# Rotary embedding of differential attention: partner rows by DMA instead of a permutation product

## The chip, the core and the metric

The kernel runs on 1 core of one Trainium2 chip. The metric is the device time of one launch in microseconds (us). Engines are called PE (matrix products), DVE (vector), ACT (scalar), POOL (GpSimd) and SP (which here only issues DMAs).

## What is computed

Two transformer blocks in float32 run on 256 tokens of width 2048. The change touches the rotary embedding of the second block, in its differential attention. There q and k are split into heads of 64 features, and the first 16 features of each head are turned in pairs that stand 8 apart:

```
rot = d // 4; half = rot // 2                       # d = 64: rot = 16, half = 8
ang = pos[:, None] * inv_freq[None, :]
x1, x2 = xr[..., :half], xr[..., half:]
rotated = concatenate([x1 * cos(ang) - x2 * sin(ang), x2 * cos(ang) + x1 * sin(ang)], axis=-1)
```

The other 48 features pass unchanged. The rotated q and k then go into two softmax attentions whose difference weighs v; a stick-breaking attention stands beside it.

## The kernel before

All large products run on PE as three products of rounded halves: a weight tile is split into a high part (`high`, L1157, on ACT, from `raw` into `w_high_low`) and a low part (`low`, L1764, on DVE). A **tick** is one piece of 256 weight rows by 512 columns: SP loads it into one of 8 `raw` slots, ACT makes its high part, DVE its low part, and PE multiplies (`tick`, L508). Eight ticks, steps 0 to 7, make a **unit**. The high and low parts have 4 buffers, so ACT may make the high part of a tick when PE has finished the tick 4 before it; ACT and DVE therefore work 3 ticks ahead. At step s of unit n each of them first makes its part of the tick 3 later, and then does what the program hangs at (n, s). This order is written out by hand, and each engine keeps it: what hangs at a step holds up every later high or low part of that engine.

The 12 units of the q, k and v projection of the second block (`for n in range(12)`, L1057 on PE, L1661 on ACT, L2557 on DVE) come in two halves of four pairs of heads each. Units 0 and 6 give q of the differential attention, 1 and 7 its k, 2 and 8 its v, the rest q, k, v of the stick-breaking attention. Units 0 to 2 and 6 to 8 collect in the two large pairs of PSUM banks, `acc`, by turns; q and k come out with features on partitions ("cols" mode), v with tokens on partitions ("rows" mode). PE may begin unit n + 2 only when unit n's pair has been emptied (`acc_free`).

The rotary part before:
- `raw_epilogue(n)` (L1582, ACT) copies both banks of unit 0, 1, 6 or 7 into `diff_q_cols` or `diff_k_cols` at step 0 of the next unit.
- `rotate(n)` (L954, PE) multiplies that copy by the signed permutation `rotate` (L118), two products of 128x512 in float32 into the emptied `acc` pair. It hangs at step 1 of units 1, 2, 7 and 8.
- `rotary(n)` (L2429, DVE) multiplies the product by the sine table and the copy by the cosine table and adds; for k it writes `diff_k_halves`. It hangs at (1, 5) for q and (2, 1) for k in the first half, at (7, 1) and (8, 1) in the second, and frees the `acc` pair at its end.

The tables are scaled by one over the root mean square of each token at (1, 5) (`rotary_tables`, L2408), from a product of PE (`root_columns`, L947).

The attentions hang beside later units: differential heads at units 3 to 5 and 9 to 11, stick-breaking heads of the first half at units 6 to 8. At (3, 0) PE begins `diff_scores(0)` (L964, the products of L974 and L977), which waits for the `acc_free` that DVE gives after `half_copy` of unit 2 (L2192, its row has L2195, into `diff_v_rows`), at DVE's step 0 of unit 3. In the stick-breaking part PE turns each head's rows by `head_turn` (L1003, its rows have L1010), for which DVE's `normed` (L2478, rows L2481) must be done. For its second and fourth head of the first half `normed` hangs at (7, 4) and (8, 4) on DVE, and `head_turn` at (7, 5) and (8, 5) on PE, after that step's tick.

Of the kernel before, what the change touches and what calls it, by code (L numbers as in the profile page):

```python
# [12 lines left out]
P = 128  # L13
# [55 lines left out]

PORTIONS = [(0, 0, 4), (0, 4, 4), (1, 0, 2), (1, 2, 2), (1, 4, 4), (0, 8, 4), (1, 8, 4), (0, 12, 4), (1, 12, 4)]  # L70
# [32 lines left out]
def constants():  # L103
# [14 lines left out]
    rot = np.zeros((P, P), np.float32)  # L118
# [3 lines left out]
    for d in range(P):  # L122
        if d % 64 < 8:
            rot[d + 8, d] = -1.0
        elif d % 64 < 16:
            rot[d - 8, d] = 1.0
# [15 lines left out]
def build(nc, ins, out):  # L142
# [147 lines left out]
    RT = att("rotary_tmp", [P, 2, TOK])  # L290
# [5 lines left out]
    RD = at("root_diagonals", [P, NT, P], F32, placed["rotary_tmp"])  # L296
# [59 lines left out]
    rot_raw, rot_full = sem("rot_raw"), sem("rot_full")  # L356
# [150 lines left out]
    def _(pe):  # L507
# [636 lines left out]
    def _(act):  # L1144
# [437 lines left out]
        def raw_epilogue(n):  # L1582
# [1255 lines left out]
```

## Time and profile before

| | |
|---|---|
| time, median of 3 runs | 2066.51 us (2066.39 to 2069.49) |
| profiled execution: span from first to last instruction | 2065.7 us |
| its time as launched | not given apart; the span lies 0.8 us under the median |
| PE busy | 2030.8 us, 98% |
| DVE busy | 1301.5 us, 63% |
| ACT busy | 974.8 us, 47% |
| share of the chain that ended last | PE 90%, DVE 6%, ACT 2% |
| 16 DMA engines, queue of SP | 55.3% busy, 173 GB/s read from HBM |
| granted clock of PE | 0.998 of full speed |

How to read it: PE's ends are modelled and its products overlap, so its pace is read from the starts of its rows. Idle time of DVE or ACT costs nothing as long as PE finds its next operand ready. Where the chain of waits runs through DVE, PE had to stand.

### The profile page before, as it was taken

Reading aid. Unit: us, or ns where it says so; the run is one execution under the profiler, and the core shown is the slowest. Engines: PE = TensorE matmul, PEld = TensorE weight load, DVE = VectorE, ACT = ScalarE, POOL = GpSimd, SP = SyncE. Lnnn points to the kernel's source line nnn. Section 1 sums busy time; section 2 is a strip of 40 time slices with the busy share of each in tenths; the row PEclk is TensorE's granted clock in tenths of the full one; section 3 lists DMA queues with packets and bytes.
Section 4 is the critical chain, followed back from the end, with each engine's and each line's share of the span. In section 5 each row is a group of like instructions: output and inputs, shape, how many; then the busy total and the mean of one; then the engine's idle time right before and its main releaser. Section 6 shows DMA issues by size and latency. Waiting matters only on the chain.

```text
span 2065.7 us, 31956 instructions
## 1 busy us (share of the span) xinstructions
PE 2030.8 (98%) x12513; PEld 1788.3 (87%) x12513; DVE 1301.5 (63%) x1770; ACT 974.8 (47%) x1414; POOL 83.7 (4%) x84
## 2 busy tenths in 40 slices
PE   8999999999999999999999999999999999999998
PEld 7898898888989898889899898888888888888886
DVE  6799776456666666658666666556546555655655
ACT  5554554344444444446445546544434434434443
POOL 2000042000000000100000001000000000000000
PEclk9999999999999999999999999999999999999999
DMA  8245576545455554755554554666666666566663
GB/s 284 93 138 188 172 213 216 171 133 173 142 160 148 154 162 133 244 169 170 161 166 152 160 155 149 200 184 191 193 189 191 191 194 185 189 196 186 189 196 105
DMA packets 202935, 360.87 MB, mean 175 GB/s; under 512 B 25360, under 2 KB 33904, under 8 KB 202160
## 3 DMA queue, kind: packets, MB, share of 16 engines
q1 hardware_dynamic: 200656, 351.88, 55.3%
q0 software_dynamic: 1664, 5.97, 0.9%
q8 instruction: 99, 1.62, 0.3%
q10 hardware_dynamic: 480, 1.10, 0.1%
q14 instruction: 36, 0.29, 0.0%
HBM read 356.03 MB, written 2.10 MB: 173 GB/s over the span
## 4 chain that ended last, share of the span: by engine, by line
PE 90%; DVE 6%; ACT 2%; issue 2%; DMA 0%; ACTq 0%; POOL 0%; DVEq 0%; POOLq 0%
PE acc L517 35%; PE acc L521 19%; PE banks L517 8%; PE banks L1113 6%; PE acc L1113 6%; PE banks L1116 3%; PE acc L1116 3%; DVE w_high_low L1764 1%; PE acc L607 1%; ACT w_high_low L1157 1%; PE banks L882 1%; PE acc L548 1%; PE banks L910 1%; PE banks L999 1%; PE banks L977 1%
## 5 line engine op out<-in xcount | busy, mean ns | idle before, releaser
L1764 DVE TENSOR_TENSOR w_high_low<-raw,w_high_low 128x1024 fp32r<-128x1024 f32 x648 | 795.1, 1235 | 611.1 <-ACT w_high_low L1157 609.8
L1157 ACT ACTIVATE w_high_low<-raw 128x1024 fp32r<-128x1024 f32 x648 | 682.0, 1059 | 735.6 <-PE acc L517 329.7
L521 PE MATMUL acc<-x_high_low,w_high_low 128*128 128x256 f32 x3648 | 454.7, 285 | 0.7 <-issue 0.7
L521 PEld LDWEIGHTS acc<-x_high_low,w_high_low 128*128 128x128 f32 x3648 | 443.9, 192 | 3.5 <-issue 2.2
L517 PE MATMUL acc<-w_high_low,x_high_low 128*128 128x512 f32 x1728 | 413.9, 396 | 1.1 <-DVE w_high_low L1764 1.1
L517 PEld LDWEIGHTS acc<-w_high_low,x_high_low 128*128 128x128 f32 x1728 | 322.1, 188 | 68.2 <-issue 1.8
L517 PE MATMUL acc<-w_high_low,h_high 128*128 128x512 f32 x1088 | 292.6, 391 | 3.0 <-DVE w_high_low L1764 1.1
L517 PEld LDWEIGHTS acc<-w_high_low,h_high 128*128 128x128 f32 x1088 | 202.7, 188 | 45.9 <-issue 2.1
L517 PE MATMUL acc<-w_high_low,h_low 128*128 128x512 f32 x544 | 167.6, 389 | 0.0
L1113 PE MATMUL acc<-x_high_low,w_high_low 128*128 128x512 f32 x512 | 161.3, 396 | 1.5 <-DVE x_rows L2117 1.1
L1113 PE MATMUL banks<-x_high_low,w_high_low 128*128 128x512 f32 x512 | 160.8, 395 | 0.0
L517 PE MATMUL banks<-w_high_low,h_high 128*128 128x512 f32 x480 | 128.3, 389 | 0.0
L517 PEld LDWEIGHTS acc<-w_high_low,h_low 128*128 128x128 f32 x544 | 102.1, 188 | 21.4
L1116 PEld LDWEIGHTS banks<-x_high_low,w_high_low 128*128 128x128 f32 x512 | 96.2, 188 | 22.7
L1116 PEld LDWEIGHTS acc<-x_high_low,w_high_low 128*128 128x128 f32 x512 | 96.2, 188 | 22.7
L517 PEld LDWEIGHTS banks<-w_high_low,h_high 128*128 128x128 f32 x480 | 90.1, 188 | 18.7
L1116 PE MATMUL acc<-x_high_low,w_high_low 128*128 128x256 f32 x512 | 100.6, 278 | 0.0
L1116 PE MATMUL banks<-x_high_low,w_high_low 128*128 128x256 f32 x512 | 100.6, 278 | 0.0
L1113 PEld LDWEIGHTS acc<-x_high_low,w_high_low 128*128 128x128 f32 x512 | 78.3, 189 | 2.6 <-DVE x_rows L2117 1.3
L1113 PEld LDWEIGHTS banks<-x_high_low,w_high_low 128*128 128x128 f32 x512 | 77.9, 189 | 0.0
L517 PE MATMUL banks<-w_high_low,h_low 128*128 128x512 f32 x240 | 73.9, 389 | 0.0
L517 PEld LDWEIGHTS banks<-w_high_low,h_low 128*128 128x128 f32 x240 | 45.0, 188 | 9.4
(362 smaller groups left out, 1635.7 us busy)
## 6 DMA issues: line engine op xcount, KB each, us to landing
raw<-in_b_w_in SPq DMA_DIRECT2D x128, 512.0 KB, 3.8
raw<-in_w_mlp_in SPq DMA_DIRECT2D x128, 512.0 KB, 3.7
raw<-in_w_mlp_out SPq DMA_DIRECT2D x128, 512.0 KB, 4.5
raw<-in_w_in SPq DMA_DIRECT2D x96, 512.0 KB, 4.0
raw<-in_kv_w SPq DMA_DIRECT2D x48, 512.0 KB, 4.1
raw<-in_a_w_in SPq DMA_DIRECT2D x32, 512.0 KB, 6.3
raw<-in_b_w_out SPq DMA_DIRECT2D x32, 512.0 KB, 4.7
raw<-in_w_out SPq DMA_DIRECT2D x32, 512.0 KB, 4.6
```

The source lines that it names most:

```text
L517: ins_ = nc.tensor.matmul(PAIRS[pair][:, t, :], xa[:, kt + j, t * P:(t + 1) * P], wa[:, k, j, :], start=first and n == 0, stop=last and n ...
L521: ins_ = nc.tensor.matmul(ACC[pair][:, m // 2, (m % 2) * TOK:(m % 2 + 1) * TOK], wa[:, k, j, m * P:(m + 1) * P], xa[:, kt + j, :], start=f ...
L548: ins_ = nc.tensor.matmul(PAIRS[pair][:, t, :], xa[:, kt, t * P:(t + 1) * P], wa[:, s % SPLIT, j, :], start=start and s == SPLIT and j == ...
L607: ins_ = nc.tensor.matmul(ACC[0][:, m // 2, (m % 2) * TOK:(m % 2 + 1) * TOK], RAW[:, s, j, m * P:(m + 1) * P], XF[kt // 8][:, kt % 8, :], ...
L882: ins_ = nc.tensor.matmul(bank[:, lo:lo + w], QT[:, h, t * P:(t + 1) * P], keys[:, g:g + 1, 0:w].rearrange("p o k -> p (o k)"), start=Fals ...
L910: ins_ = nc.tensor.matmul(BK[3][:, t * P:(t + 1) * P], PTB[:, n % 2, b * P:(b + 1) * P], v[:, k, g * HD:(g + 1) * HD], start=b < 2, stop=b ...
L977: ins_ = nc.tensor.matmul(BK[m][:, lo:lo + w], DQ[:, h, t * P:(t + 1) * P], DK[:, m, h, 0:w], start=False, stop=t == NT - 1, skip_group_ch ...
L999: ins_ = nc.tensor.matmul(BK[3][:, t * P:(t + 1) * P], cols[:, b * P:(b + 1) * P], v[:, k, h * HD:(h + 1) * HD], start=b < 2, stop=b != 1)
L1113: nc.tensor.matmul(both, WH[:, k, j, m * P:(m + 1) * P], XX[:, 2 * s + j, :, :].rearrange("p c t -> p (c t)"), start=s == 0 and j == 0, st ...
L1116: ins_ = nc.tensor.matmul(both[:, 0:TOK], WL[:, k, j, m * P:(m + 1) * P], XH[:, 2 * s + j, :], start=False, stop=s == SLOTS - 1 and j == 1 ...
L1157: nc.scalar.activation(WH[:, s % SPLIT, :, :], RAW[:, s, :, :], ACT.Copy).then_inc(hi_ready, SLOTS + 1 if first_one else 1)
L1764: V.tensor_tensor(WL[:, k, :, :], RAW[:, p % SLOTS, :, :], WH[:, k, :, :].bitcast(F32), ALU.subtract).then_inc(lo_ready, SLOTS + 1 if isin ...
```

## The change

The permutation product and its constant are gone. ACT copies only the first bank of the pair, DVE the second (a new `raw_epilogue` at step 0 of the next unit), and DVE's copy frees the pair at once. ACT then issues 8 DMAs (`partners`), each of which moves 8 partner rows of 2 KB inside SBUF from the copy into `rotary_tmp` or into a second buffer that lies in `transposed_tmp`; the sign stands in the sine table. The other rows of the sine table are zero; DVE zeroes `rotary_tmp` once, at (1, 3). `rotary` waits for the DMAs, reads the buffers instead of PSUM, and hangs at (2, 1), (2, 5), (7, 4) and (8, 4). `partners` hangs at (1, 7), (2, 3), (7, 1) and (8, 1). `diff_scores` of a half's first head waits for `rot_used` too. `root_diagonals` moves to the place of `squares`.

```
+PARTNERS_AT = [(1, 7), (2, 3), (7, 1), (8, 1)]
+ROTARY_AT = [(2, 1), (2, 5), (7, 4), (8, 4)]
...
-            cos[d], sin[d] = np.cos(angle), np.sin(angle)
-    put("rotate", rot)
+            cos[d], sin[d] = np.cos(angle), np.sin(angle) * (1 if d % 64 >= 8 else -1)
...
+    RT = [RT0, TMP[:, :, 1, :]]
...
# PE
-        def rotate(n):
-
-            pair = [G_QKV, G_QKV + 1, G_QKV + 6, G_QKV + 7][n] % 2
-            dst = (DQ, KR)[n % 2]
-            for b in range(2):
-                pe.wait_ge(rot_raw, 2 * n + b + 1)
-                ins_ = nc.tensor.matmul(ACC[pair][:, b, :], const("rotate"),
-                                        dst[:, 2 * b:2 * b + 2, :].rearrange("p m t -> p (m t)"), start=True, stop=True)
-                ins_.then_inc(rot_full, 1)
...
             if h == 0:
                 pe.wait_ge(acc_free, G_QKV + 6 * (n // 4) + 3)
+                pe.wait_ge(rot_used, 2 * (n // 4) + 2)
...
-                if s == 1 and kind in (1, 2):
-                    rotate(2 * j + kind - 1)
...
# ACT
             if n >= 2:
                 act.wait_ge(a_full, 8)
+                act.wait_ge(rot_used, n - 1)
+            nc.scalar.activation(flat(dst[:, 0:2, :]), ACC[n % 2][:, 0, :], ACT.Copy,
+                                 scale=64 ** -0.5 if n % 2 == 0 else 1.0).then_inc(rot_raw, 1)
+
+        def partners(n):
+
+            dst = (DQ, KR)[n % 2]
+            if n == 0:
+                act.wait_ge(root_cols, 1)
+            else:
+                act.wait_ge(rot_used, n)
+            act.wait_ge(rot_raw, n + 1)
+            act.wait_ge(acc_free, [G_QKV, G_QKV + 1, G_QKV + 6, G_QKV + 7][n] + 1)
             for b in range(2):
-                nc.scalar.activation(flat(dst[:, 2 * b:2 * b + 2, :]), ACC[n % 2][:, b, :], ACT.Copy,
-                                     scale=64 ** -0.5 if n % 2 == 0 else 1.0).then_inc(rot_raw, 1)
+                for lo in (0, 64):
+                    for a in range(2):
+                        act.dma_start(RT[b][lo + 8 * a:lo + 8 * a + 8, :, :],
+                                      dst[lo + 8 - 8 * a:lo + 16 - 8 * a, 2 * b:2 * b + 2, :]).then_inc(partners_in, 16)
...
+                if (n, s) in PARTNERS_AT:
+                    partners(PARTNERS_AT.index((n, s)))
...
# DVE
         def rotary(n):
+            v.wait_ge(partners_in, 128 * (n + 1))
             for b in range(2):
-                v.wait_ge(rot_full, 2 * n + b + 1)
...
-                ins_ = V.tensor_tensor(RT[:, :, :], ACC[group % 2][:, b, :].rearrange("p (m t) -> p m t", m=2),
-                                       const("sin").unsqueeze(1).to_broadcast(wide), ALU.mult)
+                ins_ = V.tensor_tensor(RT[b][:, :, :], RT[b][:, :, :], const("sin").unsqueeze(1).to_broadcast(wide), ALU.mult)
...
                 if b:
-                    ins_.then_inc(acc_free, 1)
+                    ins_.then_inc(rot_used, 1)
+                    v.wait_ge(rot_used, n + 1)
...
+        def raw_epilogue(n):
+
+            dst = (DQ, KR)[n % 2]
+            v.wait_ge(slot_used, SLOTS * (U_QKV + [0, 1, 6, 7][n] + 1))
+            v.wait_ge(rot_raw, n + 1)
+            if n >= 2:
+                v.wait_ge(a_full, 8)
+                v.wait_ge(rot_used, n - 1)
+            V.tensor_scalar(flat(dst[:, 2:4, :]), ACC[n % 2][:, 1, :], 64 ** -0.5 if n % 2 == 0 else 1.0, None,
+                            ALU.mult, ALU.bypass).then_inc(acc_free, 1)
...
                     if s == 3:
                         root()
+                        steps.inc(V.memset(RT0[:, :, :], 0.0))
...
                         rotary_tables()
-                        rotary(0)
...
-                if s == 1 and (n == 7 or kind == 2):
-                    rotary(2 * j + kind - 1)
+                if (n, s) in ROTARY_AT:
+                    rotary(ROTARY_AT.index((n, s)))
                 if kind >= 3:
                     second_stage("diff", j, 8 * (kind - 3) + s)
                 elif j:
                     second_stage("sb", j - 1, 8 * kind + s)
```

What the table of places does to each engine's order is shown at three places. The first is ACT from (1, 7) to (2, 3); `w_high_low` rows are high parts, one for each tick. Before:

```order
L1157 ACTIVATE w_high_low<-raw 128x1024 [waits slot_used,raw_in2]
L1157 ACTIVATE w_high_low<-raw 128x1024 [waits slot_used,raw_in3]
L1590 ACTIVATE diff_k_cols<-acc 128x512 [waits slot_used]
L1590 ACTIVATE diff_k_cols<-acc 128x512
L1157 ACTIVATE w_high_low<-raw 128x1024 [waits slot_used,raw_in4]
L1157 ACTIVATE w_high_low<-raw 128x1024 [waits slot_used,raw_in5]
L1579 ACTIVATE lambda_small<-lambda_small 128x2 [waits lam_dve]
L1157 ACTIVATE w_high_low<-raw 128x1024 [waits slot_used,raw_in6]
```

With the change (line numbers are those of the changed kernel, 12 lower here):

```order
L1593 DMA rotary_tmp<-diff_q_cols 8x512 [waits acc_free,rot_raw,root_cols]
L1593 DMA rotary_tmp<-diff_q_cols 8x512 x3
L1593 DMA transposed_tmp<-diff_q_cols 8x2x256 x4
L1145 ACTIVATE w_high_low<-raw 128x1024 [waits slot_used,raw_in3]
L1578 ACTIVATE diff_k_cols<-acc 128x512 [waits slot_used]
L1145 ACTIVATE w_high_low<-raw 128x1024 [waits slot_used,raw_in4]
L1145 ACTIVATE w_high_low<-raw 128x1024 [waits slot_used,raw_in5]
L1567 ACTIVATE lambda_small<-lambda_small 128x2 [waits lam_dve]
L1145 ACTIVATE w_high_low<-raw 128x1024 [waits slot_used,raw_in6]
L1593 DMA rotary_tmp<-diff_k_cols 8x512 [waits acc_free,rot_raw,rot_used]
L1593 DMA rotary_tmp<-diff_k_cols 8x512 x3
L1593 DMA transposed_tmp<-diff_k_cols 8x2x256 x4
```

Two groups of 8 DMAs stand between the high parts, and the copy of k has one row instead of two.

The second is DVE from the k rotation of the first half to the emptying of unit 2. Before, from the middle of the rotation:

```order
L2439 TENSOR_TENSOR diff_k_cols<-diff_k_cols,constants 128x512
L2443 TENSOR_TENSOR diff_k_halves<-diff_k_cols,rotary_tmp 64x512 [waits dve_steps]
L2443 TENSOR_TENSOR diff_k_halves<-diff_k_cols,rotary_tmp 64x512
L1764 TENSOR_TENSOR w_high_low<-raw,w_high_low 128x1024 [waits hi_ready] x3
L2423 TENSOR_TENSOR lambda_small<-lambda_small 128x1 [waits lam_act]
L2424 TENSOR_SCALAR lambda_small<-lambda_small 128x1 [waits dve_steps]
L2426 TENSOR_SCALAR head_gains<-head_gains 128x1 [waits hn_in]
L1764 TENSOR_TENSOR w_high_low<-raw,w_high_low 128x1024 [waits hi_ready,dve_steps]
L1764 TENSOR_TENSOR w_high_low<-raw,w_high_low 128x1024 [waits hi_ready] x3
L2195 TENSOR_SCALAR diff_v_rows<-acc,rstd 128x512 [waits slot_used,act_part]
```

With the change, from (2, 5):

```order
L1769 TENSOR_TENSOR w_high_low<-raw,w_high_low 128x1024 [waits hi_ready,dve_steps]
L2440 TENSOR_TENSOR rotary_tmp<-rotary_tmp,constants 128x512 [waits partners_in]
L2442 TENSOR_TENSOR diff_k_cols<-diff_k_cols,constants 128x512
L2446 TENSOR_TENSOR diff_k_halves<-diff_k_cols,rotary_tmp 64x512 [waits dve_steps]
L2446 TENSOR_TENSOR diff_k_halves<-diff_k_cols,rotary_tmp 64x512
L2440 TENSOR_TENSOR transposed_tmp<-transposed_tmp,constants 128x2x256 [waits dve_steps]
L2442 TENSOR_TENSOR diff_k_cols<-diff_k_cols,constants 128x512
L2446 TENSOR_TENSOR diff_k_halves<-diff_k_cols,transposed_tmp 64x512 [waits dve_steps]
L2446 TENSOR_TENSOR diff_k_halves<-diff_k_cols,transposed_tmp 64x512
L1769 TENSOR_TENSOR w_high_low<-raw,w_high_low 128x1024 [waits hi_ready,rot_used]
L1769 TENSOR_TENSOR w_high_low<-raw,w_high_low 128x1024 [waits hi_ready] x2
L2200 TENSOR_SCALAR diff_v_rows<-acc,rstd 128x512 [waits slot_used,act_part]
```

The rotation now stands behind the low part of unit 3's first tick, and three low parts follow between it and `diff_v_rows`, where before there were seven.

The third is DVE at steps 2 to 4 of unit 8. Before:

```order
L1764 TENSOR_TENSOR w_high_low<-raw,w_high_low 128x1024 [waits hi_ready]
L1789 CAST h_high<-transposed_tmp 128x256 [waits tr_tmp]
L1792 TENSOR_TENSOR h_low<-transposed_tmp,h_high 128x256 [waits dve_steps]
L1764 TENSOR_TENSOR w_high_low<-raw,w_high_low 128x1024 [waits hi_ready]
L2476 TENSOR_SCALAR head_small<-head_small 128x2 [waits ss_act]
L1764 TENSOR_TENSOR w_high_low<-raw,w_high_low 128x1024 [waits hi_ready]
L2481 TENSOR_SCALAR head_rows<-banks,head_small 128x128 [waits r_pool]
L2481 TENSOR_SCALAR head_rows<-banks,head_small 128x128
```

With the change, at step 4:

```order
L1769 TENSOR_TENSOR w_high_low<-raw,w_high_low 128x1024 [waits hi_ready]
L2440 TENSOR_TENSOR rotary_tmp<-rotary_tmp,constants 128x512 [waits partners_in]
L2442 TENSOR_TENSOR diff_k_cols<-diff_k_cols,constants 128x512
L2446 TENSOR_TENSOR diff_k_halves<-diff_k_cols,rotary_tmp 64x512 [waits dve_steps]
L2446 TENSOR_TENSOR diff_k_halves<-diff_k_cols,rotary_tmp 64x512
L2440 TENSOR_TENSOR transposed_tmp<-transposed_tmp,constants 128x2x256 [waits dve_steps]
L2442 TENSOR_TENSOR diff_k_cols<-diff_k_cols,constants 128x512
L2446 TENSOR_TENSOR diff_k_halves<-diff_k_cols,transposed_tmp 64x512 [waits dve_steps]
L2446 TENSOR_TENSOR diff_k_halves<-diff_k_cols,transposed_tmp 64x512
L2497 TENSOR_SCALAR head_rows<-banks,head_small 128x128 [waits r_pool,rot_used]
L2497 TENSOR_SCALAR head_rows<-banks,head_small 128x128
```

The k rotation of the second half (8 rows) now stands between the low part of step 4 and `head_rows`, the `normed` of the fourth head.

## Rows read from the trace of the kernel before

**Rows 1.** The page: busy us, share of the span, instructions

```profile
PE 2030.8 (98%) x12513; PEld 1788.3 (87%) x12513; DVE 1301.5 (63%) x1770; ACT 974.8 (47%) x1414; POOL 83.7 (4%) x84
```

**Rows 2.** Timeline of PE, unit 7: start us, us, engine, line, operation, tiles

```profile
1119.53 1.88 PE L960 MATMUL acc<-diff_q_cols,constants 128*128 128x512 f32 x4
1121.24 0.38 PE L1010 MATMUL banks<-constants,head_rows 128*128 128x128 f32 x2
```

**Rows 3.** Timeline of ACT, units 1 and 2; bracket: idle before, releaser

```profile
979.85 1.06 ACT L1157 ACTIVATE w_high_low<-raw 128x1024 fp32r<-128x1024 f32 x1 [2.25 <-PE acc L521]
982.73 1.06 ACT L1157 ACTIVATE w_high_low<-raw 128x1024 fp32r<-128x1024 f32 x1 [1.82 <-PE acc L521]
...
985.48 1.06 ACT L1157 ACTIVATE w_high_low<-raw 128x1024 fp32r<-128x1024 f32 x1 [0.71 <-PE acc L517]
988.20 1.06 ACT L1157 ACTIVATE w_high_low<-raw 128x1024 fp32r<-128x1024 f32 x1 [1.66 <-PE acc L517]
```

**Rows 4.** PE's waits, 940 to 1420 us: total, times, longest

```profile
PE banks L974 <- DVE diff_v_rows L2195: 0.5, 2, 0.3
```

**Rows 5.** Timeline of PE, start of unit 3

```profile
1009.29 0.45 PE L974 MATMUL banks<-causal_rounded,ident_rounded 128*128 128x384 f32 x1 [0.26 <-DVE diff_v_rows L2195]
```

**Rows 6.** Timeline of DVE, start of unit 3

```profile
1008.49 0.75 DVE L2195 TENSOR_SCALAR diff_v_rows<-acc,rstd 128x512 f32<-128x512 f32 x1
```

**Rows 7.** Timeline of DVE, units 1 and 2

```profile
978.18 0.69 DVE L2436 TENSOR_TENSOR rotary_tmp<-acc,constants 128x512 f32<-128x512 f32 x1
...
982.16 3.49 DVE L1764 TENSOR_TENSOR w_high_low<-raw,w_high_low 128x1024 fp32r<-128x1024 f32 x3
985.57 0.28 DVE L2418 TENSOR_TENSOR lambda_rows<-lambda_rows 128x128 f32<-128x128 f32 x1
...
989.00 0.69 DVE L2436 TENSOR_TENSOR rotary_tmp<-acc,constants 128x512 f32<-128x512 f32 x1 [1.20 <-PE acc L960]
...
994.52 3.50 DVE L1764 TENSOR_TENSOR w_high_low<-raw,w_high_low 128x1024 fp32r<-128x1024 f32 x3
997.93 0.16 DVE L2423 TENSOR_TENSOR lambda_small<-lambda_small 128x1 f32<-128x1 f32 x1
...
998.19 0.14 DVE L2426 TENSOR_SCALAR head_gains<-head_gains 128x1 f32<-128x1 f32 x1
```

**Rows 8.** DMAs ACT issues: one at the start, the two last stores

```profile
1.68 0.48 ACTq L1184 DMA_DIRECT2D log_dt_rows<-in_a_log_dt  x1
...
L1746 ACTq DMA_DIRECT2D out<-x_rows x2: 369/372/375, 2056.5 to 2061.5; - x2
```

**Rows 9.** SP's 16 KB DMAs inside SBUF, landing; last: a weight tile

```profile
L455 SPq DMA_DIRECT2D u_phases<-u_cols x48: 586/597/1580, 47.9 to 110.0; - x48
...
DMA to landing us min/median/max: 1.8/1.8/3.1
...
raw<-in_w_in SPq DMA_DIRECT2D x96, 512.0 KB, 4.0
```

**Rows 10.** Line 2356, DVE empties one bank: ns min/median/max

```profile
L2356 DVE TENSOR_SCALAR q_cols<-acc x4: 691/692/693, 425.7 to 753.4; 128x512 f32<-128x512 f32 x4
```

**Rows 11.** Timeline of ACT, units 7 and 8

```profile
1120.31 1.04 ACT L1157 ACTIVATE w_high_low<-raw 128x1024 fp32r<-128x1024 f32 x1
...
1128.13 1.06 ACT L1157 ACTIVATE w_high_low<-raw 128x1024 fp32r<-128x1024 f32 x1 [1.36 <-PE acc L521]
...
1156.55 1.06 ACT L1157 ACTIVATE w_high_low<-raw 128x1024 fp32r<-128x1024 f32 x1 [1.25 <-PE acc L517]
```

**Rows 12.** Timeline of DVE, step 4 of unit 8

```profile
1157.73 1.22 DVE L1764 TENSOR_TENSOR w_high_low<-raw,w_high_low 128x1024 fp32r<-128x1024 f32 x1
1159.54 0.61 DVE L2481 TENSOR_SCALAR head_rows<-banks,head_small 128x128 f32<-128x128 f32 x2 [0.58 <-POOL head_small L2784]
```

**Rows 13.** Timeline of PE: line 1010 in units 7 and 8

```profile
1135.14 0.38 PE L1010 MATMUL banks<-constants,head_rows 128*128 128x128 f32 x2
...
1161.73 0.38 PE L1010 MATMUL banks<-constants,head_rows 128*128 128x128 f32 x2
```

More of the change, by code:

```diff
@@ L94 @@
 _at = 0
-for _name, _width in [("ident", P), ("steps", 16), ("causal", 3 * P), ("rotate", P), ("strict", P), ("later", P), ("ones", P),
+for _name, _width in [("ident", P), ("steps", 16), ("causal", 3 * P), ("strict", P), ("later", P), ("ones", P),
                       ("cos", TOK), ("sin", TOK), ("cmp_bias", NT * 16), ("cmp_valid", NT * 16)]:
@@ L117, in constants @@
     put("ones", np.ones((P, P), np.float32))
-    rot = np.zeros((P, P), np.float32)
     inv_freq = (np.float32(500000.0) ** (-np.arange(0, 16, 2, dtype=np.float32) / np.float32(16))).astype(np.float32)
@@ L122, in constants @@
     for d in range(P):
[L123 to L126, printed above, removed]
         if d % 64 < 16:
             angle = pos * inv_freq[d % 8]
-            cos[d], sin[d] = np.cos(angle), np.sin(angle)
-    put("rotate", rot)
+            cos[d], sin[d] = np.cos(angle), np.sin(angle) * (1 if d % 64 >= 8 else -1)
     put("cos", cos)
@@ L289, in build @@
     SA, SB, SC = (at(f"stick_{x}", [P, 2, 384], F32, placed[y]) for x, y in zip("abc", ("probs_first", "probs_second", "mixed_cols")))
-    RT = att("rotary_tmp", [P, 2, TOK])
+    RT0 = att("rotary_tmp", [P, 2, TOK])
     ON = att("head_rows", [P, 2, NT, HD])
@@ L295, in build @@
     KR = att("diff_k_cols", [P, 4, TOK])
-    RD = at("root_diagonals", [P, NT, P], F32, placed["rotary_tmp"])
+    RT = [RT0, TMP[:, :, 1, :]]
+    RD = at("root_diagonals", [P, NT, P], F32, placed["squares"])
     LAM4 = at("lambda_rows", [P, 4, 64], F32, base + 206 * K1)
@@ L354, in build @@
     z_tanh, z_used = sem("z_tanh"), sem("z_used")
-    rot_raw, rot_full = sem("rot_raw"), sem("rot_full")
+    rot_raw, partners_in, rot_used = sem("rot_raw"), sem("partners_in"), sem("rot_used")
     a_full, b_full, c_full = sem("a_full"), sem("b_full"), sem("c_full")
@@ L2429, in rotary @@
         def rotary(n):
-            group = [G_QKV, G_QKV + 1, G_QKV + 6, G_QKV + 7][n]
             dst = (DQ, KR)[n % 2]
+            v.wait_ge(partners_in, 128 * (n + 1))
             for b in range(2):
-                v.wait_ge(rot_full, 2 * n + b + 1)
                 d = dst[:, 2 * b:2 * b + 2, :]
                 wide = [P, 2, TOK]
-                ins_ = V.tensor_tensor(RT[:, :, :], ACC[group % 2][:, b, :].rearrange("p (m t) -> p m t", m=2),
-                                       const("sin").unsqueeze(1).to_broadcast(wide), ALU.mult)
+                ins_ = V.tensor_tensor(RT[b][:, :, :], RT[b][:, :, :], const("sin").unsqueeze(1).to_broadcast(wide), ALU.mult)
                 steps.inc(ins_)
@@ L2442, in rotary @@
                         half = slice(64 * m, 64 * m + 64)
-                        ins_ = V.tensor_tensor(DK[half, m, 2 * b:2 * b + 2, :], d[half, :, :], RT[half, :, :], ALU.add)
+                        ins_ = V.tensor_tensor(DK[half, m, 2 * b:2 * b + 2, :], d[half, :, :], RT[b][half, :, :], ALU.add)
                         if m == 0:
@@ L2446, in rotary @@
                 else:
-                    ins_ = V.tensor_tensor(d, d, RT[:, :, :], ALU.add)
+                    ins_ = V.tensor_tensor(d, d, RT[b][:, :, :], ALU.add)
                 if b:
-                    ins_.then_inc(acc_free, 1)
+                    ins_.then_inc(rot_used, 1)
+                    v.wait_ge(rot_used, n + 1)
                 else:
                     steps.link(ins_)
+        def raw_epilogue(n):
[7 more added lines that the diff above has]
+                            ALU.mult, ALU.bypass).then_inc(acc_free, 1)
         def qkv_epilogue(n):
@@ L2455, in qkv_epilogue @@
             if kind < 2:
+                raw_epilogue(2 * j + kind)
                 return
```

## The prediction

> **What bounds the kernel now.** I read the page's busy shares first. PE is busy 98% of the span, DVE 63%, ACT 47% [rows 1]. So only two things can change the time: what PE computes, and how long PE stands for an operand. The timelines around the change come next. In unit 7 the two permutation products begin at 1119.53 and the next product, line 1010, at 1121.24 [rows 2]: they hold PE for 1.71 us, with nothing beside them on PE. Then PE's own waits: over the whole attention part there is one on the path of this change, before `diff_scores`, for DVE's `diff_v_rows`, 0.26 us in unit 3 and again in unit 9 [rows 4, 5]. That wait is small, but it shows a place without slack: DVE ends that row at 1008.49 + 0.75 and PE goes on at 1009.29 [rows 5, 6]. What delays DVE there delays PE by as much. Last I read how far ACT and DVE run ahead: the high parts start one tick apart, 2.88 us in unit 1 and 2.72 in unit 2 [rows 3], each freed by PE and not by ACT.
>
> **The change, part by part.** Times below are on the clock of the trace of before; where rotations of PE are gone I subtract 1.71 us for each.
>
> *Removed from PE.* Four times two products: 4 x 1.71 = 6.85 us, all on the path.
>
> *Emptying the banks.* ACT loses one copy of two, DVE gains one, 0.69 us [rows 10]. It stands in front of low parts that are early: one starts about 1.1 us after its high part and takes 1.2, three ticks (8.2 us) ahead of PE, so some 5.9 us are spare. It also frees the `acc` pair earlier than now. Cost nothing; if DVE had no lead it would be 4 x 0.6 = 2.4 us. The zeroing at (1, 3), one write of 128x512, is not shown; it lies between nothing and 0.7 us (a copy of that size), under the same cover. I take nothing.
>
> *The issue of the DMAs.* ACT issues 4 x 8, and its next high part stands behind them. The trace has no such DMA. The nearest rows are ACT's own: 0.48 us for a small one at the start, 0.37 for a store of 128 long rows [rows 8]. SP's 16 KB moves inside SBUF, of the same size but of 256-byte pieces, took 0.60 for an issue [rows 9]. With some 0.04 us between two issues the ends are 0.41 and 0.64 us for each. I take 0.48 in all, near ACT's rows, so 3.84 us for a group of 8. A DMA here has 8 partition rows. The Trainium skill ("DMA: Bandwidth & Descriptors", Why a DMA increments its semaphore by 16) says that such a copy runs on as many engines as divide its row count, here 8, and that the issuing sequencer itself writes the rest of the 16 increments. That speaks for the dearer end; by it the sum below, at 0.64 us for an issue, would come out above zero.
>
> *First half, place by place.* The high part of tick (2, 2) starts at 979.85 - 1.71 = 978.14 [rows 3]. I let the issues begin with it, since they don't need ACT's datapath (if they wait for its end, all below is 1.0 later): 978.2 to 982.0. The next high part, due at 982.73 - 1.71 = 981.0, runs from 982.0 to 983.1. DVE follows: low part 1.14 (three take 3.49, the last of them 1.22 [rows 7]), the new copy 0.6, the lambda sums 0.6 (0.28 and a second row like it [rows 7]), low part 1.14, then the q rotation, which takes 982.16 - 978.18 = 3.98 [rows 7], to 990.6. ACT could issue the k group at 988.20 - 1.71 + 2.72 = 989.2, but must wait for this rotation (`rot_used`): 990.65 to 994.5. Then its high part 1.06 to 995.55, DVE's low part to 996.7, the lambda rows 0.45 (997.93 to 998.33 [rows 7]) to 997.15, the low part of unit 3's first tick to 998.3. Only now comes the k rotation, 994.52 - 989.00 = 5.52 [rows 7], to 1003.8. Behind it stand three low parts, 3.4, to 1007.2, and `diff_v_rows`, 0.75, to 1008.0. PE is through its first tick at 1009.29 - 0.26 - 3.42 = 1005.6, and waits 2.45 us instead of 0.26. **Cost: 2.2 us.** Before, the k rotation stood four steps earlier and DVE had caught up. Cheapest: with 0.41 us for an issue, 1.1 us. Dearest: with 0.64, 4.75, and 5.8 if the issues also wait for the high part.
>
> *Second half, unit 7.* PE turns the second head's rows at 1135.14 - 1.71 = 1133.4 [rows 13] and needs `normed`, which now stands behind the q rotation at (7, 4). ACT's high part of 1120.31 [rows 11] is followed by the issues, to 1124.2, a head copy 0.4, a high part 1.06, the squares 0.9, two high parts 2.1: 1128.6, where it was due at 1128.13 - 1.71 + 1.06 = 1127.5. Low part 1.14, rotation 3.98, `normed` 0.61 [rows 12]: 1134.3, a wait of 0.9. If ACT issues while its queued work still waits, before 1120, the group is covered and the wait is nothing. I take 0.4 us, between nothing and 2.1 (issues at 0.64).
>
> *Unit 8.* Here the 5.5 us of the k rotation stand ahead of `normed` of the fourth head. The high part of step 4 comes at 1156.55 - 3.42 = 1153.1 [rows 11], ends at 1154.2, the low part takes DVE to 1155.3, the rotation to 1160.85, `normed` to 1161.5. PE is ready for line 1010 at 1161.73 - 3.42 = 1158.3 [rows 13]. **Cost: 3.2 us.** This does not depend on the issues: PE frees that high part itself. Before, `normed` began at 1159.54, 2.2 us ahead of PE. Bounds: 3.0 to 3.5.
>
> Every wait of PE here is lost, since PE has no idle time later in which to win it back.
>
> *Sum:* -6.85 + 2.2 + 0.4 + 3.2 = **-1.05 us**. The span of 2065.7 us lies 0.8 under the median; the difference goes on the median: 2066.5 - 1.05, about **2065.5 us**. With the cheap ends it is 2064 (-6.85 + 1.1 + 0 + 3.0 = -2.75), with the dear ends 2071 (-6.85 + 5.8 + 2.1 + 3.5 = +4.55).
>
> **Rivals.**
> *The waits don't come.* The DVE rows behind which I place PE's waits could be covered, if ACT and DVE run further ahead than the three ticks I read. For it: PE's waits are now near zero. Against it: every high part in rows 3 and 11 starts when PE frees its buffer, so there is no more lead to be had. With both gone the time is 2066.5 - 6.85 = 2059.7; with only the wait in unit 8 gone, -1.05 - 3.2, 2062.3.
> *Slower: the issue on ACT becomes the bound.* SP's slowest issue of this kind took 1.58 us [rows 9]. At 1.0 us for each, 16 issues on the chain of the first half add 16 x 0.52 = 8.3 us, in unit 7 and unit 8 together some 4.9: +12, 2078.7. It decides from about 0.73 us for an issue, where the sum passes +4. For it: 8 rows in a burst behind a full queue of weight tiles. Against it: the median was 0.60, and ACT's own rows are lower.
> *The partner rows land late.* The k group is issued by 994.5 and wanted at 998.3, 3.8 us later; SP's small moves landed in 1.8 us, at most 3.1, but a weight tile in 4.0 [rows 9]. The Trainium skill (same page, Issuing engines are not separate DMA queues) says that all issuers end on the same 16 engines, so small rows interleave with the weight tiles; no row of this kind was beside such a stream. At 4.0 us it costs 0.2; at 6 us, 2.2 in the first half, +1.2 in all, 2067.7.
>
> **How the numbers follow.** Forecast 0.66; no waits, or only one, 0.17; issue as the bound 0.10; late landing 0.07. A measurement of this kernel can tell about 0.2%, 4.1 us. Of the forecast nearly all lies within that, as does late landing and the share of the first rival that loses one wait only in part. Faster by over 0.2% (under 2062.4): 0.16. Slower (over 2070.6): 0.11. Within: 0.73. The range takes the cheap end and a little of the first rival, and the dear end less its far corner: 2061.8 to 2069.8.
>
> **What would show it.** The 8 permutation products (16 rows of PE) are gone. PE's list of waits shows `diff_scores` behind `diff_v_rows` with about 2.7 us in unit 3 and still 0.3 in unit 9, and line 1010's successor in unit 8 with about 3.2 behind `head_rows`. ACT's DMAs take about 0.45 us each and land in 2 to 3. The forecast is wrong if either wait is missing, if ACT's issues take over 0.7 us, or if PE stands anywhere else.

## The result and the profile after

| | before | after |
|---|---|---|
| median, 4 runs each | 2067.82 us (2066.39 to 2069.49) | 2079.75 us (2078.23 to 2081.43) |
| profiled span | 2065.7 us | 2076.8 us |
| PE busy | 2030.8 us | 2028.8 us |
| PE's waits, all | 26.3 us | 39.5 us |
| granted clock, mean | 0.998 | 0.996 |

The ratio is 1.0058 (95% interval 1.0045 to 1.0070): the change costs about 12 us. The forecast was 2065.5 us within 2061.8 to 2069.8, "within 0.2%" with a chance of 0.73. It was wrong in size and in sign.

PE's own waits in the kernel after, the longest kinds (what it waited for, then us in all, times, longest):

```profile
PE banks L1000 <- DVE head_rows L2497: 7.2, 2, 4.9
PE banks L590 <- DMA x_rows<-in_x: 6.3, 1, 6.3
PE banks L964 <- DVE diff_v_rows L2200: 5.6, 2, 5.3
PE banks L700 <- ACT tap_blocks L1265: 3.6, 4, 2.5
PE acc L516 <- DVE w_high_low L1769: 3.2, 4, 1.1
```

The second and fourth stand in the profile of before as well. The third answers to [rows 4]: 0.5 us has become 5.6. The first is new. These are the places that the prediction named; beyond them PE only waits once more than before, 1.1 us for a low part. I call such a wait of PE a stand. In PE's timeline the stands are the numbers in brackets (idle before, and what ended it):

```profile
1003.74 3.03 PE L520 MATMUL acc<-x_high_low,w_high_low 128*128 128x256 f32 x24
1012.07 0.69 PE L964 MATMUL banks<-causal_rounded,ident_rounded 128*128 128x384 f32 x1 [5.30 <-DVE diff_v_rows L2200]
1012.56 1.48 PE L967 MATMUL banks<-diff_k_halves,diff_q_cols 128*128 128x128 f32 x4
1013.48 0.88 PE L964 MATMUL banks<-causal_rounded,ident_rounded 128*128 128x384 f32 x1
...
1141.16 0.44 PE L1000 MATMUL banks<-constants,head_rows 128*128 128x128 f32 x2 [2.27 <-DVE head_rows L2497]
...
1171.33 0.69 PE L1000 MATMUL banks<-constants,head_rows 128*128 128x128 f32 x2 [4.90 <-DVE head_rows L2497]
```

The same rows show a second loss. Behind the stand of 5.30 us the four products of L967 take until 1013.48, 0.92 us; behind a short stand they take 0.47 (below, at 1006.78). The windows of the profile (us, PE, PEld, DVE, ACT and POOL busy, then the granted clock, DMA share, GB/s) say why:

```profile
1000.00:1010.00 10.00, 5.88 (x36) 5.19 (x36) 9.73 (x15) 4.06 (x5) 0.00 (x0) 1.00 0.37 107
1012.00:1017.00 5.00, 4.93 (x18) 4.57 (x19) 1.26 (x5) 1.58 (x7) 0.00 (x0) 0.50 0.61 220
1018.00:1030.00 12.00, 12.00 (x101) 11.95 (x100) 6.12 (x10) 4.27 (x9) 0.69 (x1) 1.00 0.44 132
1171.00:1175.00 4.00, 3.67 (x11) 3.01 (x12) 2.86 (x6) 1.42 (x2) 0.00 (x0) 0.57 0.32 98
```

The granted clock is at its lower level (1.2 of 2.4 GHz) from 1010.7 to 1017.6 us and again from 1171.2 to 1174.6. PE computes in 5.5 and 3.3 us of these, so about 2.8 + 1.6 = 4.4 us are lost. Behind the stand of 2.27 us it did not fall. The Trainium skill ("TensorE: Matmul & The Clock Gate", Part 1) says that a monitor gates PE's clock by how busy PE has been. The trace agrees: both falls here came within a long stand, at 1010.7 (PE idle since 1006.8) and 1171.2 us (idle since 1166.4).

The account, for the two profiled executions: -6.85 for the products, +13.2 of waits (39.5 - 26.3), +4.4 of clock, together +10.8 us, against +11.1 in the spans and about +12 in the runs.

Where the waits come from is in the timeline of ACT, unit 1 to 2 (start, us, then the row):

```profile
977.72 1.06 ACT L1145 ACTIVATE w_high_low<-raw 128x1024 fp32r<-128x1024 f32 x1 [2.25 <-PE acc L520]
977.82 3.27 ACTq L1593 DMA_DIRECT2D rotary_tmp<-diff_q_cols  x4
981.12 2.94 ACTq L1593 DMA_DIRECT2D transposed_tmp<-diff_q_cols  x4
984.17 1.06 ACT L1145 ACTIVATE w_high_low<-raw 128x1024 fp32r<-128x1024 f32 x1 [5.39 <-PE acc L516]
...
992.75 2.70 ACTq L1593 DMA_DIRECT2D rotary_tmp<-diff_k_cols  x4
995.49 2.93 ACTq L1593 DMA_DIRECT2D transposed_tmp<-diff_k_cols  x4
998.52 3.91 ACT L1145 ACTIVATE w_high_low<-raw 128x1024 fp32r<-128x1024 f32 x4 [8.68 <-issue]
```

A group of 8 holds ACT for 5.7 to 6.6 us: 0.71 us for each transfer in the k group (992.75 to 998.42), 6.2 us in all for the q group, whose first issue took 1.26. The profile names PE as the releaser of the high part at 984.17, but the last issue ends 0.1 us before it: here the name is wrong and the row above it right. DVE follows (timeline, unit 2 to 3):

```profile
992.75 2.36 DVE L1769 TENSOR_TENSOR w_high_low<-raw,w_high_low 128x1024 fp32r<-128x1024 f32 x2
999.61 1.22 DVE L1769 TENSOR_TENSOR w_high_low<-raw,w_high_low 128x1024 fp32r<-128x1024 f32 x1 [4.50 <-ACT w_high_low L1145]
...
1001.19 1.22 DVE L1769 TENSOR_TENSOR w_high_low<-raw,w_high_low 128x1024 fp32r<-128x1024 f32 x1
1002.33 0.68 DVE L2440 TENSOR_TENSOR rotary_tmp<-rotary_tmp,constants 128x512 f32<-128x512 f32 x1
...
1007.86 3.50 DVE L1769 TENSOR_TENSOR w_high_low<-raw,w_high_low 128x1024 fp32r<-128x1024 f32 x3
1011.27 0.75 DVE L2200 TENSOR_SCALAR diff_v_rows<-acc,rstd 128x512 f32<-128x512 f32 x1
```

That is the prediction's chain, link by link. From the end of the first group on every link is later than forecast, and `diff_v_rows` ends at 1012.0 where 1008.0 was forecast.

In unit 8 ACT's k group stands in the way too. These are the end of the group on ACT, and the next low part on DVE, which had no high part until then:

```profile
1156.51 2.93 ACTq L1593 DMA_DIRECT2D transposed_tmp<-diff_k_cols  x4
1161.00 1.23 DVE L1769 TENSOR_TENSOR w_high_low<-raw,w_high_low 128x1024 fp32r<-128x1024 f32 x1 [4.65 <-ACT w_high_low L1145]
```

### The profile page after: what moved, and what is told of

Read it like the earlier page. It is cut to its first block, busy times and chain, and to the rows that moved or that the text cites. A ratio compares the mean times of both kernels' runs of the same rounds, so it can differ in the third digit from the quotient of the medians.

```text
span 2076.8 us, 31967 instructions
## 1 busy us (share of the span) xinstructions
PE 2028.8 (98%) x12497; PEld 1788.5 (86%) x12497; DVE 1304.2 (63%) x1775; ACT 971.5 (47%) x1410; POOL 83.2 (4%) x84
## 4 chain that ended last, share of the span: by engine, by line
PE 86%; DVE 7%; ACT 3%; issue 2%; ACTq 1%; DMA 0%; POOL 0%; DVEq 0%; POOLq 0%
PE acc L516 33%; PE acc L520 18%; PE banks L516 8%; PE banks L1101 6%; PE acc L1101 6%; PE banks L1104 3%; PE acc L1104 3%; DVE w_high_low L1769 2%; PE acc L606 1%; ACT w_high_low L1145 1%; ACTq L1593 1%; PE banks L881 1%; PE acc L547 1%; PE banks L909 1%; PE banks L967 1%
```

## The experiments

All times are against runs of the kernel before on the same chip. The runs of before spread over some 4 us. Two causes show in the profiled executions of the 13 kernels. PE's first 16 products of `x_cols` took 4.4 to 6.5 us. And near 100 us, at a stand of 2.5 us that every kernel has there, the clock went to its lower level for 6.8 us (in six), 3.4 us (in four) or not at all (in three). What is under 2 us is therefore read from waits.

**Take the transfers away.**

```
-            for b in range(2):
-                for lo in (0, 64):
-                    for a in range(2):
-                        act.dma_start(RT[b][lo + 8 * a:lo + 8 * a + 8, :, :],
...
-            v.wait_ge(partners_in, 128 * (n + 1))
```

The 32 transfers and DVE's wait for them are left out, so the rotation works on zeros or old rows in place of the partner rows.

> The changed kernel with ACT's 32 DMAs left out, and DVE's wait for them; all else stays in place. What it leaves out: the partner rows, so the sine term of the rotation is missing. Issue theory: the 0.71 us that each of the 32 DMAs holds ACT is what made the waits long. Then the wait before diff_scores in unit 3 falls from 5.3 to about 1.0 us, that in unit 7 to 0, that in unit 8 to 3.2, the clock stays at full speed beside them, and the kernel comes to before - 6.85 + 0.75 + 3.2 = 2.9 us under before. Order theory (the rival): the rotation stands too late in DVE's order whatever ACT does; the three waits stay as they are (5.3, 2.3, 4.9) and the kernel stays about 11 us over before.

Ratio 0.9999 (0.9990 to 1.0008), no change, where the whole change costs 12 us. The order theory falls, and the waits came as the issue theory has them: 1.1 us ahead of `diff_scores(0)`, none in unit 7, 3.1 in unit 8. The gain of 2.9 us did not come, because of the clock (a wait, then PE's row behind the stand of unit 8, then a window):

```profile
PE banks L964 <- DVE diff_v_rows L2195: 1.4, 2, 1.1
1161.62 0.69 PE L1000 MATMUL banks<-constants,head_rows 128*128 128x128 f32 x2 [3.08 <-DVE head_rows L2491]
```

```profile
1161.00:1167.00 6.00, 5.38 (x14) 4.33 (x15) 3.55 (x6) 1.42 (x2) 0.00 (x0) 0.50 0.41 107
```

With a stand of 3.1 us comes the lower level, from 1160.9 to 1167.7, which costs 3 us more (half of the 6.1 us in which PE computes). So even without a single transfer the change, as it is ordered, is worth nothing: it gains 6.85 and gives 4 back in waits and 3 in clock.

**Take only the products away.**

```
-                if s == 1 and kind in (1, 2):
-                    rotate(2 * j + kind - 1)
...
-                v.wait_ge(rot_full, 2 * n + b + 1)
+                v.wait_ge(rot_raw, 2 * n + b + 1)
```

The permutation isn't computed; DVE multiplies what stands in the banks.

> The kernel before without PE's eight permutation products; DVE multiplies the unpermuted bank by the sine table instead (what it leaves out: the permutation). This prices the gain alone: 4 x 1.71 = 6.85 us under before, between 6.3 and 7.3. If PE's time there were partly hidden, less than 5.

Ratio 0.9972 (0.9962 to 0.9982), -5.8 us (-7.9 to -3.7), with the waits of before (26.3 us in all). That is about a microsecond short of what I expected, but 6.85 lies within the interval: the first term of the prediction holds.

**Put the rotation behind the attention work in units 7 and 8.**

```
-                if (n, s) in ROTARY_AT:
-                    rotary(ROTARY_AT.index((n, s)))
                 if kind >= 3:
                     second_stage("diff", j, 8 * (kind - 3) + s)
                 elif j:
                     second_stage("sb", j - 1, 8 * kind + s)
+                if (n, s) in ROTARY_AT:
+                    rotary(ROTARY_AT.index((n, s)))
```

> The changed kernel with one thing moved: at (7, 4) and (8, 4) DVE does the attention's work (normed above all) first and the rotation after it. Theory: the waits of line 1000's successor for head_rows (2.3 and 4.9 us) go, and with the second the stretch at half clock (3.4 us of it, 1.7 us lost); up to 1 us comes back before the first ticks of units 8 and 9. So 7 to 9 us under the changed kernel, 3 to 5 us over before. Rival: the waits only move to the low parts of the next unit, and it stays within 2 us of the changed kernel.

Ratio 1.0044 (1.0031 to 1.0058), +9 us where I expected +3 to +5; from the changed kernel it can't be told apart. The waits for `head_rows` are gone, but a low part is late by 2.95 us in their place, the first half's 5.3 us stay, a new wait of 1.5 us stands in unit 9, and the clock falls twice. So the rival is nearer: a whole rotation of 4 or 5.5 us does not fit behind one tick either, and moving it within the step moves the wait.

**Issue the same transfers from SP.** SP issues them between weight tiles, at (3, 3), (3, 7), (8, 5) and (9, 5).

```
+        issue_at = {(3, 3): 0, (3, 7): 1, (8, 5): 2, (9, 5): 3}
+                if (n, s) in issue_at:
+                    partners(issue_at[n, s])
```

> The changed kernel with the same 32 DMAs issued by SP, between its loads of weight tiles, at the places that answer to ACT's. Issue theory: ACT and DVE are as free as with no DMAs, SP has more than 10 us to spare before a weight tile is missed: 2.9 us under before, waits 1.0, 0 and 3.2 us. Rival: the partner rows land late behind the weight tiles; then DVE's rotation waits for DMA and the waits of PE stay over 4 us each.

Ratio 1.0049 (1.0035 to 1.0062). The expectation failed, and the rival is near: PE's stands are 6.3, 2.3 and 3.1 us. ACT's timeline is free of issues, but SP (which keeps its order too, and stands at each weight tile for a slot) came to them late, and DVE stood for the rows:

```profile
983.38 2.83 SPq L499 DMA_DIRECT2D rotary_tmp<-diff_q_cols  x4
986.25 2.95 SPq L499 DMA_DIRECT2D transposed_tmp<-diff_q_cols  x4
989.24 8.17 SPq L416 DMA_DIRECT2D raw<-in_w_in  x4
997.52 2.72 SPq L499 DMA_DIRECT2D rotary_tmp<-diff_k_cols  x4
```

```profile
1004.58 0.69 DVE L2442 TENSOR_TENSOR rotary_tmp<-rotary_tmp,constants 128x512 f32<-128x512 f32 x1 [4.85 <-DMA transposed_tmp<-diff_k_cols]
```

An issue costs SP what it costs ACT (5.8 us a group). Taking the issues off ACT, with SP at these places, cures nothing.

**4 transfers a group, of 4 KB rows,** on ACT's queue at the change's places.

```
-            for b in range(2):
-                for lo in (0, 64):
-                    for a in range(2):
-                        act.dma_start(RT[b][lo + 8 * a:lo + 8 * a + 8, :, :],
...
+            for lo in (0, 64):
+                for a in range(2):
+                    act.dma_start(RW[lo + 8 * a:lo + 8 * a + 8, :, :],
+                                  dst[lo + 8 - 8 * a:lo + 16 - 8 * a, :, :]).then_inc(partners_in, 16)
```

> The change with 4 transfers a group instead of 8, each of 8 rows with 4 KB instead of 2 KB (16 in all, the same bytes), into one buffer of its own place; DVE zeroes 1024 columns of it once more ahead of the second half. Theory A, the price is per transfer (0.71 us of ACT each in the change's trace): a group takes ACT 2.9 us instead of 5.7 to 6.6, so the tick behind it comes some 3 us earlier. PE's stand of 5.3 us ahead of diff_scores(0) shrinks to 2.5 to 3.5 us, that of unit 8 (4.9 us) to about 3.5, unit 7's is at most 1, and what the clock loses (5.1 us in the change) is 1.7 to 5. Time against before: -6.9 + 3 + 3.5 + 0.5 + 3.4 = +3.5 us (0 to +6). Theory B, the price goes with the bytes: issues of 1.3 to 1.4 us, no stand shorter, about the change's +12 us.

Ratio 1.0 (0.9991 to 1.0009). The price goes by the transfer: 4 of 32 KB hold ACT as long (2.67 us) as 4 of 16 KB did (2.70 and 2.93).

```profile
990.77 2.67 ACTq L1593 DMA_DIRECT2D partner_rows<-diff_k_cols  x4
993.54 1.06 ACT L1146 ACTIVATE w_high_low<-raw 128x1024 fp32r<-128x1024 f32 x1 [2.68 <-issue]
```

That is theory A, and better than its numbers (I had +3.5, with 2.5 to 3.5 us at `diff_scores(0)`). PE's waits are those of the run without transfers, 1.1 us at `diff_scores(0)` and 3.1 in unit 8, and so is the time. In this order of work 16 issues cost nothing that can be measured (to some 2 us) against none; 32 cost 12 us.

**A stand by itself.** In the kernel before, 4 or 8 operations that change nothing are put on DVE ahead of `diff_v_rows` of unit 2.

```
+                for _ in range(4 if n == 2 else 0):
+                    steps.link(V.tensor_tensor(RT[:, :, :], RT[:, :, :], RT[:, :, :], ALU.max))
                 half_copy(U_QKV + n, G_QKV + n, (DV if kind == 2 else SV)[:, 1, :], RSTD[:, 1:2])
```

> The kernel before with 4 more operations of 0.69 us each on DVE ahead of diff_v_rows of unit 2 and nothing else: PE's stand ahead of diff_scores(0) becomes 0.3 + 2.8 = about 3 us. Theory A, a stand costs its length and, where it is long enough, the clock: the two stands of about 3 us seen so far differ (3.1 us was followed by 6.8 us at half clock, 2.3 us by none), so +2.8 us if the clock holds and +4.5 to +6.2 us if it falls for 3.4 or 6.8 us. Theory B, a stand costs its length only, and the falls come from elsewhere: +2.8 us and no fall at 1010 us. Theory C, PE makes part of a stand good later: less than +2.8 us.

> The same with 8 operations: a stand of 0.3 + 5.5 = 5.8 us at the same place, with none of the change in the program. Theory A: the granted clock is at half for 6.8 us right behind it as in the change's trace at 1010.7 us, which costs 3.4 us more, so +8.9 us in all. Theory B: +5.5 us and no fall. Theory C: less than +5.5 us.

With 4, ratio 1.0029 (1.0017 to 1.0042), +6.0 us; with 8, 1.0040 (1.0026 to 1.0054), +8.3 us. Timelines of PE, then a window behind the stand, for 4 operations:

```profile
1013.78 0.44 PE L974 MATMUL banks<-causal_rounded,ident_rounded 128*128 128x384 f32 x1 [3.17 <-DVE diff_v_rows L2195]
1014.06 0.86 PE L977 MATMUL banks<-diff_k_halves,diff_q_cols 128*128 128x128 f32 x4
1014.52 0.72 PE L974 MATMUL banks<-causal_rounded,ident_rounded 128*128 128x384 f32 x1
1015.04 1.49 PE L977 MATMUL banks<-diff_k_halves,diff_q_cols 128*128 128x128 f32 x4
```

```profile
1014.00:1018.00 4.00, 4.00 (x18) 3.77 (x18) 1.24 (x4) 1.70 (x8) 0.00 (x0) 0.59 0.00 2
1022.00:1030.00 8.00, 8.00 (x70) 8.00 (x68) 3.09 (x4) 3.01 (x7) 0.08 (x1) 1.00 0.62 199
```

and for 8:

```profile
1017.77 0.69 PE L974 MATMUL banks<-causal_rounded,ident_rounded 128*128 128x384 f32 x1 [6.07 <-DVE diff_v_rows L2195]
```

```profile
1014.00:1018.00 4.00, 0.23 (x1) 0.23 (x2) 3.54 (x6) 0.00 (x0) 0.00 (x0) 0.51 0.08 32
1018.00:1022.00 4.00, 4.00 (x19) 3.70 (x20) 1.24 (x4) 1.03 (x5) 0.00 (x0) 0.64 0.00 0
```

The fall comes with the stand, with nothing of the change in the program: theory B (+2.8 us, no fall) is out, and C with it. With 4 operations the pace of L977 halves in the middle (0.46 us, then 0.92). With 8 the clock is already low from 1014.1, while PE still stands, up to 1020.9; only the 3.1 us in which PE computes cost something. That gives 2.9 + 1.7 = 4.6 us and 5.8 + 1.6 = 7.4 us, each about a microsecond under the runs and within their intervals. My +8.9 counted the whole stretch.

**SP issues early, the rotation in halves.** SP's places are (2, 5), (3, 1), (8, 2) and (9, 1); each rotation is cut into its two banks, in two ticks, behind the step's attention work.

```
-ROTARY_AT = [(2, 1), (2, 5), (7, 4), (8, 4)]
+ROTARY_AT = [(2, 0), (2, 1), (2, 4), (2, 5), (7, 5), (7, 6), (8, 4), (8, 5)]
...
+                if (n, s) in ROTARY_AT:
+                    i = ROTARY_AT.index((n, s))
+                    rotary(i // 2, [i % 2])
```

> The change with its 32 transfers issued by SP as early as their data are there (by the trace at about 977, 992, 1125 and 1158 us, where SP in the run before this one issued at 983, 997, 1130 and 1158), and with the rotation cut into halves of 2.1 us that DVE does in two ticks each, behind the attention work of the tick. Theory A, the loss is made of PE's stands and the clock behind them, and both come from where the issues and rotations stand: no wait of PE over 2 us, no fall of the clock but at the start and the end, and the time is the one without the products, 2063 us or about 6 us under before (waits of 1 to 2 us in all left over, so -6 to -4). Theory B, the transfers or SP's share in them have a cost of their own wherever they stand (late weight tiles, slower tiles): not under before, with DVE and ACT waiting for weight tiles near 1000 and 1130 us.

Ratio 0.9981 (0.9972 to 0.9990), -3.9 us. One stand of 2 us is left:

```profile
1006.50 0.44 PE L983 MATMUL banks<-causal_rounded,ident_rounded 128*128 128x384 f32 x1 [2.03 <-DVE diff_v_rows L2202]
1006.78 0.82 PE L986 MATMUL banks<-diff_k_halves,diff_q_cols 128*128 128x128 f32 x4
1007.25 0.53 PE L983 MATMUL banks<-causal_rounded,ident_rounded 128*128 128x384 f32 x1
```

Theory A holds, at the edge of its numbers: the waits are 28.5 us in all and the clock does not fall behind one of them. The stand goes back to DVE, which waited for the partner rows of k:

```profile
995.62 0.69 DVE L2443 TENSOR_TENSOR rotary_tmp<-rotary_tmp,constants 128x512 f32<-128x512 f32 x1 [2.16 <-DMA transposed_tmp<-diff_k_cols]
```

**Which part cures it?** Three runs, all with the rotation's new places: the change's 32 transfers on ACT; 16 long ones on ACT; 16 long ones on SP.

> The change with its transfers left on ACT's queue at the places they have there (32 of them), and only the rotation moved as in the run that beat both kernels: in halves, in two ticks each, behind the attention work of the tick. Theory A, ACT's 5.7 us of issues ahead of the high parts of ticks (2,3) and (8,1) are what makes the stands, since the high part waits for them: the stand ahead of diff_scores(0) stays, shorter by what the cut halves give (3 to 5.5 us), that of unit 8 comes down to 0 to 2 us since head_turn's rows come ahead of the rotation, and the clock falls once. Against before: -6.9 + 3.0 to 5.5 + 1 + 3.4 = +0.5 to +3 us. Theory B, the place of the rotation is all: the time of the run that beat both, 5 to 6 us under before.

> The same places of the rotation, with the transfers on ACT's queue and 4 of them a group, of 4 KB rows (16 in all). If the price is per transfer and the stands come from the issues together with the rotation's place, both are taken away by half and by all here: PE's wait ahead of diff_scores(0) about 1 us, none over 1 us in units 7 and 8, no fall of the clock near 1010 or 1160 us, -6 to -5 us against before. If SP's queue is needed for it: about 0, as with 4 transfers and the rotation where the change has it.

> The run that beat both kernels (SP issues, halves) with 4 transfers a group. There DVE waited 2.2 us for k's partner rows at 995 us, and PE then 2.0 us ahead of diff_scores(0). 4 transfers are issued 2.8 us sooner, so DVE's wait goes, and PE's falls to 0 to 0.5 us: 1.5 to 2 us less than that run, so -7.5 to -7 us against before. The extra zeroing on DVE (about 1 us at tick (6,3)) lies in its idle time, or else takes 0.5 to 1 us of this back.

| | ratio (95%) | waits | longest at the change's places |
|---|---|---|---|
| 32 on ACT | 1.0051 (1.0037 to 1.0065) | 37.8 us | 3.6, 2.6, 2.2 |
| 16 on ACT | 0.9979 (0.9970 to 0.9988) | 28.2 us | 1.1, 1.0 |
| 16 on SP | 0.9972 (0.9961 to 0.9982) | 26.3 us | 0.4, 0.3 |

With 32 on ACT the group still ends late, whatever the places of the rotation (ACT's timeline, then DVE's):

```profile
997.42 2.93 ACTq L1593 DMA_DIRECT2D transposed_tmp<-diff_k_cols  x4
1000.45 3.90 ACT L1145 ACTIVATE w_high_low<-raw 128x1024 fp32r<-128x1024 f32 x4 [8.67 <-issue]
```

```profile
1001.54 1.23 DVE L1769 TENSOR_TENSOR w_high_low<-raw,w_high_low 128x1024 fp32r<-128x1024 f32 x1 [4.49 <-ACT w_high_low L1145]
```

For 32 on ACT I had expected +0.5 to +3 us and it is +10.5: the stand at `diff_scores(0)` came as expected (3.6), but stands in unit 8 (2.2 and 1.2), one in unit 9 (2.6) and late low parts (2.5 in all) came on top. Its profiled execution accounts for some +6.4 of it (-6.85 + 11.5 of waits + 1.7 of clock) and was also 2.5 us faster than the median of its runs. Another 1.7 us of that execution's time lay in its start, before any of the change runs; the rest stays open. The two others behaved as forecast in their waits. In time each gained about a microsecond less than I gave, 4.3 us for at least 5 and 5.8 for at least 7, within their intervals. With 16 on SP, PE's wait at `diff_scores(0)` is back at the 0.26 us of [rows 5]:

```profile
1008.37 0.44 PE L983 MATMUL banks<-causal_rounded,ident_rounded 128*128 128x384 f32 x1 [0.26 <-DVE diff_v_rows L2204]
```

This version beats both kernels: 5.8 us under before, all that the products were worth in the run that merely dropped them. The three versions under before can't be told from each other by their intervals.

Put together: the rotation's new places alone give +10.5 us, half the issues alone (the run with 4 KB rows) 0, both together -4.3. So both are needed, and SP's queue is not. Whether the cut into halves or the place behind the attention work does the rotation's part was not tried apart.

## Why the prediction was wrong

- *Removed from PE, -6.85.* Right within the interval; -5.8 measured.
- *The issue of the DMAs, "I take 0.48 in all".* **This step failed.** It is 0.71 us, above even the dear end of 0.64, so that a group costs 5.7 us and not 3.84. That is past the 0.7 which the prediction set as a sign of being wrong. I went by ACT's own rows [rows 8], a small load at the start and two large stores; the nearest in kind, the 16 KB moves inside SBUF [rows 9], gave 0.60, and the rule of the Trainium skill that I cited spoke for the dearer end. Why 8 rows are dearer than a long store was not tried.
- *First half, "Cost: 2.2 us".* The chain was right in each link. With 16 issues 0.23 us dearer it gives 3.7 us more, 5.9; measured are 5.0 ahead of `diff_scores` and 1.1 one tick before, 6.1. (The signs named about 2.7 us for this wait, the working 2.45; 5.3 came.) The run without transfers shows what of it belongs to the order alone: 0.9.
- *Unit 7, 0.4.* Measured 2.3, above the dear end of 2.1; none without the transfers, so it is from the same price.
- *Unit 8, "This does not depend on the issues".* **Wrong.** 3.1 us without them, 4.9 with them: the k group ends at 1159.44, and DVE had to wait until 1161.00 for the next high part, where the forecast had it ready. I had read that PE frees that high part, and not what else stands on ACT's queue.
- *"Every wait of PE here is lost".* True, and not enough. **The clock is missing from the sum:** about 4.4 us in the change. No row of before had a stand of 3 us beside the attention work. But its own profile has a fall of 3.4 us, from 100.1 to 103.5 us, behind a stand of 2.5 us (rows below), and a forecast with a wait of 3.2 us in it should have named the risk. In the run without transfers that very stand lost 3 us more.
- *The rivals.* "The issue on ACT becomes the bound" gave 2078.7 at 1.0 us each, "from about 0.73". The result is close to it, with 0.71 and the clock in place of 1.0. It had a chance of 0.10; since the first half's dear end alone was 4.75 us, it should have had more. The 0.73 is misworked too: by this rival's own figures (8.3 + 4.9 us for 0.52 more an issue) the sum passes +4 at 0.68 us, and at 0.71 it is +4.8. Late landing played no part on ACT's queue; DVE waited for partner rows only where SP issued them (up to 4.9 us late in the order, 2.2 early).

With what was measured in each place the sum is -6.85 + 6.1 + 2.3 + 4.9 + 4.4 = +10.9 us. The fall of the clock in the profile of before (PE's timeline, then a window; its granted clock, 0.91, comes ahead of the last two numbers):

```profile
98.51 1.81 PE L701 MATMUL banks<-u_cols,tap_blocks 128*128 128x192 f32 x12 [2.47 <-ACT tap_blocks L1277]
90.00:110.00 20.00, 16.99 (x178) 16.13 (x168) 18.59 (x25) 13.04 (x19) 0.00 (x0) 0.91 0.16 41
```

## What to carry to other kernels

Count the transfers that an engine with other work issues, not their bytes, and price them by the row of the same kind; half as many and twice as long turned +12 us into nothing. Work that must be done once, like a rotation of 4 us on DVE, did best here in pieces of 2 us behind the work of a tick, with its DMAs issued as soon as their data were there. On this kernel, which is bound by PE, a stand of 3 us cost about 6, since the clock fell with it, while four of five stands of 2.0 to 2.6 us beside the attention work brought no fall. Whether two short waits are better than one long one of the same sum was not tried. The run with 4 KB rows warns against it as a rule: at 319.8 us its clock fell for 3.4 us behind two waits of 0.7 and 1.0 us, 2.2 us from start to start, which the other kernels have too, without a fall.

## What I had not expected of the hardware

- The granted clock was at 1.2 GHz behind every stand of 2.9 us or more beside the attention work (2.95, 3.1, 3.1, 3.1, 3.2, 3.6, 4.9, 5.3, 5.3, 6.1, 6.3 us), for 3.4 or 6.8 us by the records. With eight of them (all but 2.95, 3.2 and 3.6) it had fallen before PE went on. Length of stand and length of fall don't go together: 3.1 us was followed once by 3.4 and twice by 6.8. Of the shorter ones, 2.0, 2.2, 2.3 and 2.6 were followed by none, but one of 2.3 (transfers on SP) by 3.4; and the stand of 2.5 us near 97 us went with 0, 3.4 or 6.8 us.
- A transfer of 8 partition rows inside SBUF took ACT 0.63 to 0.70 us to issue where the buffer takes its rows whole, 0.70 to 0.76 where they land in two pieces of 1 KB (`transposed_tmp`), and 1.3 us for two of the 32. Rows of 4 KB cost the same as rows of 2 KB, and SP pays what ACT pays (0.62 to 0.76, and 0.79 for its first).
